# Four small sums moved two products later in VectorE's order in a Strassen-like feed-forward stage

## The reference

```
h2 = rms_norm(x1, norm2_g) * (1.0 + scale2) + shift2
ff = (jax.nn.silu(h2 @ w_gate) * (h2 @ w_up)) @ w_down
y = x1 + gate2 * ff
```

## Time and profile before

| what | us |
|---|---|
| median of 3 runs | 2680.95 |
| lowest and highest | 2677.6, 2681.61 |
| the profiled execution | 2676.8 |
| its span | 2675.0 |
| TensorE busy in it | 2568.2 (96%) |
| VectorE busy | 1982.7 (74%) |
| ScalarE busy | 1284.8 (48%) |
| GpSimd busy | 499.4 (19%) |

### The profile page before, as it was taken

One profiled execution on the slowest core, in us unless ns is written; L12 is line 12 of the kernel. 1 busy time (PEld: TensorE's weight loads), 2 busy tenths in 40 slices (PEclk: granted clock), 3 DMA queues, 4 the chain that ended last, 5 costly groups with the idle time before them and its releaser, 6 DMA issues.

```text
span 2675.0 us, 46742 instructions
## 1 busy us (share of the span) xinstructions
PE 2568.2 (96%) x17757; PEld 2210.4 (83%) x17757; DVE 1982.7 (74%) x3672; ACT 1284.8 (48%) x2509; POOL 499.4 (19%) x621
## 2 busy tenths in 40 slices
PE   5999999999999999999799999989999999999998
PEld 3678887777787778878799999978889999998787
DVE  6647887557767548677899999956588899886546
ACT  4212221338789646656454545534445555554343
POOL 2106787440001000000113222110000000000000
PEclk8999999999999989999899999999999999999999
DMA  9663333853433896444799779897568867888664
GB/s 338 200 203 113 122 122 134 292 173 123 129 120 111 321 362 215 145 147 135 239 320 283 246 246 290 266 313 238 192 213 268 249 213 220 266 262 288 232 216 159
DMA packets 407081, 583.52 MB, mean 218 GB/s; under 512 B 35105, under 2 KB 295969, under 8 KB 396866
## 3 DMA queue, kind: packets, MB, share of 16 engines
q1 hardware_dynamic: 383144, 440.50, 51.0%
q0 software_dynamic: 21264, 139.16, 15.6%
q10 hardware_dynamic: 2450, 0.87, 0.1%
HBM read 447.76 MB, written 199.27 MB: 242 GB/s over the span
## 4 chain that ended last, share of the span: by engine, by line
PE 64%; DVE 7%; ACT 3%; issue 2%; DMA 1%; SPq 1%; DVEq 0%; ACTq 0%
PE f_ps L2869 27%; PE f_ps L2911 15%; PE c_ps_w L2165 7%; PE a_o_ps L406 2%; PE a_s_ps L377 2%; PE a_t_ps L388 2%; DVE f_ws L3055 2%; PE c_ps_glu L2140 2%; PE b_ps_t L1787 1%; ACT a_probs L444 1%; PE a_o_ps L414 1%; PE b_ps_s L1799 1%; PE b_ps_o L1824 1%; DVE f_s L3063 1%; PE a_t_ps L357 1%
## 5 line engine op out<-in xcount | busy, mean ns | idle before, releaser
L2869 PE MATMUL f_ps<-f_x,f_ws 128*128 128x256 f32 (+1 forms) x7392 | 906.6, 285 | 33.4 <-DVE f_sl L3118 20.1
L2869 PEld LDWEIGHTS f_ps<-f_x,f_ws 128*128 128x128 f32 x7392 | 901.2, 191 | 45.0 <-issue 38.9
L2911 PE MATMUL f_ps<-f_ws 128*128 128x512 f32 x1848 | 423.9, 391 | 12.6 <-DVE f_ws L3055 9.2
L2911 PEld LDWEIGHTS f_ps<-f_ws 128*128 128x128 f32 x1848 | 348.7, 189 | 88.4 <-DVE f_ws L3055 9.6
L946 PE MATMUL p_out_ps<-p_w,p_hT 128*128 128x512 f32 x1620 | 379.8, 392 | 1.1 <-DVE p_qk L1222 1.1
L3055 DVE TENSOR_TENSOR f_ws<-f_raw,f_ws 128x1024 fp32r<-128x1024 f32 x208 | 268.1, 1295 | 132.6 <-ACT f_ws L2972 132.4
L946 PEld LDWEIGHTS p_out_ps<-p_w,p_hT 128*128 128x128 f32 x1620 | 300.9, 188 | 73.1 <-issue 11.6
L3055 DVE TENSOR_TENSOR f_ws<-raw,f_ws 128x1024 fp32r<-128x1024 f32 x210 | 262.7, 1257 | 117.7 <-ACT f_ws L2972 117.4
L2972 ACT ACTIVATE f_ws<-raw 128x1024 fp32r<-128x1024 f32 x210 | 220.9, 1057 | 210.7 <-PE f_ps L2911 106.8
L2972 ACT ACTIVATE f_ws<-f_raw 128x1024 fp32r<-128x1024 f32 x208 | 218.8, 1057 | 215.0 <-PE f_ps L2911 106.6
L444 ACT ACTIVATE a_probs<-a_probs,a_o 128x256 f32<-128x256 f32 (+1 forms) x384 | 171.1, 451 | 1.4 <-DVE a_o L487 1.4
(11 more groups left out here) (381 smaller groups left out, 3800.5 us busy)
## 6 DMA issues: line engine op xcount, KB each, us to landing
scratch_aF<-f_stage SPq DMA_DIRECT2D x44, 896.0 KB, 6.6
out_dram<-in_cache_k_dram POOLq DMA_DIRECT2D x8, 4088.0 KB, 14.7
out_dram<-in_cache_v_dram POOLq DMA_DIRECT2D x8, 4088.0 KB, 14.5
raw<-in_w_gate_dram SPq DMA_DIRECT2D x88, 256.0 KB, 5.3
raw<-in_w_up_dram SPq DMA_DIRECT2D x88, 256.0 KB, 5.5
f_raw<-in_w_gate_dram SPq DMA_DIRECT2D x88, 256.0 KB, 5.3
f_raw<-in_w_up_dram SPq DMA_DIRECT2D x88, 256.0 KB, 5.7
raw<-scratch_aF SPq DMA_DIRECT2D x78, 256.0 KB, 3.3
```

The costliest lines, as they stand in the source:

```text
L2869: mm = pe.matmul(ps[bank][:, 0:w], ws[s % SLOTS][:, y, j * 512 + k * 128:j * 512 + (k + 1) * 128], x_half(b, p, z)[:, k], start=(p < 3 and ...
L2911: mm = pe.matmul(ps[bank][:, :], slot[:, y, j * 128:(j + 1) * 128], slot[:, z, 512:1024], start=(p < 3 and k == 0 and x == 0), stop=(k == ...
```

## The change

The call of `stage_sums` moves from behind product 1 to behind product 3 of VectorE's loop over the products of a pair. Nothing is added or left out. It concerns 40 of the 44 pairs: in the first pair of a round (0 and 22) there is none, and the stage sums of the last pair of blocks 1 and 3 stand apart and stay.

```diff
                         fill_lo(slot_of(b, n, p) + SLOTS)
-                        if p == 1 and pair:
+                        if p == 3 and pair:
                             stage_sums(b * NPAIRS + n - 1)
```

## The result

The changed kernel takes 2693.21 us (median of five runs, 2688.61 to 2698.48), the kernel before in the same session 2680.95 (2677.6 to 2685.21). The ratio is 1.0051, 95% interval 1.0033 to 1.0070: slower by 0.5%, some 13.7 us (0.0051 x 2681). The forecast was 2688.1 with a range of 2677 to 2695. The stage sums move in 42 pairs (1 to 21 and 23 to 43), not in 40 as the description and the prediction count. The profiled execution took 2692.78 us, 16.0 more than that of before; its span is 2691.0 against 2675.0.

The account below looks back on a forecast made before the run. TensorE was taken to bound the kernel, except in pairs of blocks 0 and 1 where the C22 sum is late. Terms 2.5 + 2.5 + 1.2 + 1.25 - 0.5 + 0.2 = 7.15 us on 2680.95 gave 2688.1, range 2677 to 2695.

Parts of the forecast that it names:

- The bound and its limit: Undisturbed even pairs, blocks 0 and 1: C22 sum ends at 16.89, limit 16.61, so TensorE loses 0.28 us a pair.
- The first rival: Even pairs pay nothing and GpSimd's later start costs half: 0 to 4 us, say 2682.5; chance 0.26.
- GpSimd's start: Pairs 13 and 19: GpSimd starts 1.19 us later, at 4.49, and each pair gets 1.25 us longer.
- Pairs 15 and 17: Blocks 0 and 1: GpSimd starts near 5.8 behind cache moves; 0.3 us more for each pair.
- Pairs 7 and 9: GpSimd's long row difference would stop a low part instead of a stage sum: 0.5 us less for both.
- Pair 11: Among pairs 1, 10 and 11: VectorE has no gap up to the C22 sum in either order, so no cost.
- Blocks 2 and 3: Block 2 costs nothing, C22 sum at 17.67 under a limit of 17.73; block 3 costs 0.2 us.
- the 0.06 us of room: Block 2: the margin by which the C22 sum was to stay within its limit of 17.73.
- The stores: A store's landing is asked for most of a pair later; 0.7 us in pair 3, 0.2 us in block 3.
- more than forecast: Rival: block 2 pays 1.8 us, block 3's store waits 3, slow clock 1.7, giving 2694.6; chance 0.13.
- The size: Whole kernel: the terms sum to 7.15 us on the profiled 2676.8.
- The range: Whole kernel: 2677 to 2695 us.

Follow-up runs that it names:

- e7: Kernel before without the eight GpSimd cache moves of blocks 0 and 1: 2669.93 us, ratio 0.9970 to the kernel before.
- e8: Changed kernel without the eight GpSimd cache moves of blocks 0 and 1: 2678.88 us, ratio 1.0000 to the kernel before.
- e10: Kernel before, with GpSimd in blocks 0 and 1 also waiting for the first half of product 1: 2689.34 us, ratio 1.0049.
- e1: Kernel before with the stage sums moved behind the fourth product in blocks 2 and 3 only: 2677.89 us against 2677.42, ratio 1.000.
- e3: Kernel before with the stage sums moved in the odd pairs of blocks 0 and 1 only: 2680.43 us, ratio 1.0012.
- e4: Kernel before with the stage sums put behind the third product's low part in all pairs, one product later: 2685.32 us, ratio 1.0030.
- e11: Changed kernel, GpSimd in blocks 0 and 1 waiting for three multiplies and the end of product 0: 2686.90 us, ratio 1.0043 to the kernel before.
- e2: Kernel before with the stage sums moved in the even pairs of blocks 0 and 1 only: 2690.64 us, ratio 1.0049.
- e9: Kernel before, with GpSimd waiting for three of four multiplies in blocks 0 and 1 only: 2663.14 us against 2676.51, ratio 0.9948.
- e6: Kernel before, with GpSimd waiting for three of four multiplies in all blocks: 2681.84 us, ratio 1.0020.
- e5: Changed kernel, with GpSimd waiting for three of four multiplies in all blocks: 2702.21 us, ratio 1.0090 to the kernel before.

## Why the prediction was right, and where it was not

- **The bound and its limit** held. The C22 sum ends at 16.88 to 16.89 in undisturbed even pairs (forecast 16.89), and 0.28 a pair was 0.27. The first rival held that such a small lateness lies inside the scatter of the marks; in e7 and e8, free of other disturbance, the nine pairs gave 0.23 to 0.28.
- **GpSimd's start** held: 4.50 in pair 13, forecast 4.49, and 1.23 and 1.11 us in pairs 13 and 19, forecast 1.25 each. In e8 against e7, where pair 13 waits for no store, it was 1.10. e10, which delays GpSimd and moves nothing else, shows the cause.
- **Pairs 15 and 17** were expected to get 0.3 us each longer; in the profiled execution they changed by 0.11 and -0.54. The cost has a shape that the prediction missed. Pairs that wait for no store took 20.13 us with GpSimd's first subtraction at 3.29 (before, pair 19), 20.75 at 3.97 (changed, pair 17), 21.13 at 4.33 (e10, pair 19), 21.29 at 4.52 (before, pair 15) and 21.47 at 5.83 (e10, pair 15): about 1 us per us up to 4.5, then nearly flat. In pairs 15 and 17 the move had put the start at 4.52 already in the kernel before, so the cost was paid there, and the step to 5.75 in pair 15 added only 0.11. In pair 17 the stop in pair 16 let GpSimd start at 3.97, and that is the gain of 0.54. Without the moves both start at 3.29 and go to 4.49, and they cost 1.14 and 1.10 as the others.
- **Pairs 7 and 9** should have given back 0.5; pair 7 did (-0.50), pair 9 lost 0.66, and without the moves both lost 0.3. The term was wrong in sign, 0.7 us in sum. Pair 11's 0.66 is not there in e8 against e7. It is the clock: TensorE stops for 4.30 us in both kernels, and the granted clock behind the stop is 0.52 for 3 us and 0.91 for the next 3 before, 0.50 and 0.69 after. Why it came back later was not found.
- **Blocks 2 and 3** held, and e1 shows it: 1.000. The C22 sum of pair 25 ends at 17.66 (forecast 17.67), and the 0.06 us of room were enough.
- **The stores** are the step that failed. The prediction said that a store's landing is asked for most of a pair later, and gave the stores 0.7 us in pair 3 and 0.2 in block 3. That is untrue in even pairs of blocks 0 and 1, and in pair 5: the multiply waited for a store seven times, 15.0 us in all. The rival "more than forecast" had the mechanism but put it into block 3. In pair 16 of the kernel before, the multiply began 10.5 us after the pair's start without a wait. The timelines of ScalarE (starts of pairs 15 and 16) and VectorE there:

```profile
1619.66 1.06 ACT L2972 ACTIVATE f_ws<-f_raw 128x1024 fp32r<-128x1024 f32 x1 [1.78 <-PE f_ps L2869]
...
1640.96 1.06 ACT L2972 ACTIVATE f_ws<-raw 128x1024 fp32r<-128x1024 f32 x1 [1.59 <-PE f_ps L2869]
```

```profile
1651.48 0.42 DVE L3135 TENSOR_TENSOR f_stage<-f_sl,f_cu 128x256 f32<-128x256 f32 x1
```

  SyncE's queue and then GpSimd's issue show what changed, each of the kernel before and then of the changed one (an issue's duration is how long the queue was held):

```profile
1629.25 9.96 SPq L2619 DMA_DIRECT2D f_raw<-in_w_up_dram  x1
...
1643.98 1.11 SPq L2671 DMA_DIRECT2D scratch_aF<-f_stage  x1
```

```profile
1635.64 12.48 SPq L2619 DMA_DIRECT2D f_raw<-in_w_up_dram  x1
...
1652.88 1.11 SPq L2671 DMA_DIRECT2D scratch_aF<-f_stage  x1
```

```profile
1623.16 0.52 POOL L2746 DMA_DIRECT2D out_dram<-in_cache_k_dram  x1 [17.96 <-DVE f_stage L3135]
```

```profile
1631.77 0.52 POOL L2746 DMA_DIRECT2D out_dram<-in_cache_k_dram  x1 [19.43 <-DVE f_stage L3135]
```

  The cache move leaves 4.7 us after the start of pair 15 instead of 3.5. A load held in SyncE's queue gets through 16.1 us after the move in the one kernel (1639.21 - 1623.16) and 16.4 in the other (1648.12 - 1631.77). It is the moves that hold it: in e7 and e8, without them, no such load in pairs 1 to 21 was held for more than 3.4 us. The store behind it leaves 4.4 us after the start of pair 16 instead of 3.0. It then lands after 10.9 us instead of 7.1 by the two DMA records, at 15.4 instead of 10.1. And the multiply asks 1.4 us sooner, since the stage sums no longer stand ahead of it: 1.4 + 3.8 + 1.4, less the 0.3 that it had to spare, is the wait of 6.3 us. The slow clock behind the stop of 4.26 then adds 2.0.
- **The size.** On the profiled execution 7.15 us were forecast and 16 found. Pair 16 is 6.2 of the 8.9 missing, pair 5 most of the rest: its multiply waits 1.8 us for a store, and the slow clock stands behind its stop. e3 and e4 have pair 5 at 23.5 to 23.7 us too. On the medians the mechanism without stores was 8 to 9 us and the stores some 5.
- **The range** held partly by luck. Its upper part, in which 2693.21 lies, stood for a rival with 1.8 us in block 2 and 3 us in block 3, and those blocks cost nothing (e1). The stores that did cost were in blocks 0 and 1.

The two landings of pair 16's store differ by 3.8 us, and the place of the move does not settle that. In kernels with the move issued at 3.4 to 3.5 of pair 15 the store landed 9.8 to 10.4 after the start of pair 16 (e4, before, e3, e1) but also 13.1 (e11); with the move at 4.7 to 4.8 it landed at 14.1 to 15.4 (e10, e2, changed); in e9, with the move 0.9 us ahead of pair 15, at 11.8. What does sort these cases is another transfer. In every even pair of blocks 0 and 1 GpSimd also issues a load of 1 MB for the down projection. In pair 16 of the kernel before, then of the changed one:

```profile
1645.66 0.72 POOL L2765 DMA_DIRECT2D f_wq<-in_w_down_dram  x1 [12.58 <-DVE f_stage L3135]
```

```profile
1653.15 0.73 POOL L2765 DMA_DIRECT2D f_wq<-in_w_down_dram  x1 [12.25 <-DVE f_stage L3135]
```

The store left 1.7 us ahead of this load before, and 0.3 us ahead in the changed kernel. The traces of the eleven kernels with all moves hold 33 stores that pairs 2, 16 and 18 ask for. The nine that left 1.2 us or more ahead of the load took 6.3 to 7.6 us to land; the thirteen that left at most 0.5 us ahead of it or up to 1.0 behind took 9.1 to 11.6; the eleven in between, 0.6 to 1.0 ahead, took 5.8 to 10.5. In e11 the load leaves 1.3 us sooner together with GpSimd and so comes 0.75 us behind the store (10.5 us). In e10 and the changed kernel the load keeps its place and the store comes later. Two edits thus bring the two transfers together in different ways, and both give the late landing; the three stores of e6 in block 3 did the same with a cache move. This is read from the traces laid side by side: no run moved the load alone, and what happens between 0.6 and 1.0 us stays open.

## What to carry to other kernels

Before work is moved behind an engine's idle time, look for who else counts the instruction that now comes later: here the price of 0.27 us in the pair itself was small beside the 1.1 us in the next pair, paid because GpSimd waited for one multiply more than its place needed. A wait for a transfer that no one notices in the profile before has a margin too, and it must be read (asked at, landed at) like the room of any other wait. Read also how far ahead of the next bulk transfer the small one leaves: 1.7 us was enough here and 0.3 was not. Loosen such a wait stage by stage: the same edit was worth -14.5 us in one stage and +19.7 in another.

## What the runs showed of the hardware

- A subtraction of GpSimd (128x512) lengthens an operation of VectorE with two inputs in SBUF by 1.09 us: a weight sum from 1.22 to 2.31, a stage sum from 0.42 to 1.51. The sums with an input in PSUM that meet one stay at 0.41 to 0.42. The page "SBUF — State Buffer" of the Trainium skill, section "Who interferes with whom", says that a VectorE instruction with two SBUF inputs contends with a GpSimd instruction that reads SBUF and that one with at most one such input does not, and the rows agree.
- So it matters where in a pair GpSimd's 8 us lie. From 3.3 to 4.5 us each us of later start made an odd pair about 1 us longer, from 4.5 to 5.8 only 0.2 in all, and with a start at 0.4 (e9, pair 13) even the 0.25 us that this pair paid before were gone.
- A cache move issued by GpSimd holds a load in SyncE's queue: seven of the eight moves in blocks 0 and 1 held one for 8.9 to 12.5 us in the kernel before and the changed one; without the moves none was held over 3.4 us (e7, e8).
- A store that leaves at most 0.5 us ahead of a bulk transfer of GpSimd, or up to 1 us behind it, landed late in every case: after 9.1 to 11.6 us beside a load of 1 MB, after 18.2 to 19.8 beside a cache move in block 3 (e5, e6), where 4 to 9 us is usual.
- The length of a stop of TensorE did not settle the clock behind it: 0.58 behind 1.98 us, 1.00 behind 2.24, 0.50 behind 3.37, in one execution. Behind a stop of 4.30 us in pair 11, the same in both kernels, the clock over the second 3 us was 0.91 in one and 0.69 in the other.
